# Two transformer-like blocks in one launch: five places where the order or the grain of small steps is changed

## The reference, cut to what matters

```python
def reference(x, c, ..., mem_2, ...):
    x = first_block(x, c, w_ada, b_ada, w_in, ...)     # below
    return second_block(x, mem_2, w_in_2, ...)         # below

# first block: six vectors of 1024 from silu(c) @ w_ada + b_ada scale, shift and gate what follows
#   h = norm(x) * (1 + scale) + shift;  in-projection of h
#   retention: 4 heads of 128, rotary, per-head decay, head norm, gate
#   gated linear attention: 4 heads in 2 pairs
#   out-projection, norm, MLP with squared ReLU (1024 -> 4096 -> 1024), norm

# second block:
#   proj = h @ w_in_2, split into z, xbc, dt, u_s5, x_rg, g_rg
def ssd_mixer(z, xbc, dt_raw, conv_w, conv_b, dt_bias, a_log, d_skip, norm_w):
    xbc = silu(causal_dwconv(xbc, conv_w, conv_b))     # 4 taps, per channel, along the tokens
    dt  = softplus(dt_raw + dt_bias);  a = -exp(a_log)
    # per chunk of 128 tokens and head: y = (C B' * exp(segment sums of dt*a)) (x*dt)
    #   + C (decayed state), state carried from chunk to chunk; then + x*d_skip, * silu(z), norm
def s5_mixer(u, lam_re, lam_im, log_step, b, c, d_skip, glu_w, glu_b):
    lam_bar = exp(lam * step);  b_bar = ((lam_bar - 1) / lam) * b      # complex
    h = linear_scan(lam_bar, b_bar u);  y = gelu(real(c h) + d_skip * u)
    return y * sigmoid(y @ glu_w + glu_b)
#   RG-LRU mixer; y = concat(ssd, s5, rg) @ w_out_2, norm, cross-attention, norm, MLP, norm
```

## Time and profile before

| | |
|---|---|
| median of three executions | 2831.02 us |
| lowest and highest | 2827.89, 2831.63 us |
| profiled execution, its own time | 2834.3 us |
| its span in the profile | 2832.5 us |
| mean granted clock of TensorE | 0.971 |
| TensorE busy | 2664.0 us (94%), 13340 matmuls |
| TensorE's weight loads busy | 1375.1 us (49%) |
| VectorE busy | 1434.6 us (51%) |
| ScalarE busy | 966.8 us (34%) |
| GpSimd busy | 686.9 us (24%) |
| HBM | 64 GB/s over the span |

### The profile page before, as it was taken

One profiled execution on the slowest core, in us unless ns is written; L12 is line 12 of the kernel. 1 busy time (PEld: TensorE's weight loads), 2 busy tenths in 40 slices (PEclk: granted clock), 3 DMA queues, 4 the chain that ended last, 5 costly groups with the idle time before them and its releaser, 6 DMA issues.

```text
span 2832.5 us, 34001 instructions
## 1 busy us (share of the span) xinstructions
PE 2664.0 (94%) x13340; PEld 1375.1 (49%) x13340; DVE 1434.6 (51%) x2282; ACT 966.8 (34%) x1152; POOL 686.9 (24%) x355
## 2 busy tenths in 40 slices
PE   6999999888999999999988899888999999999998
PEld 3677766443444444444454444344544444444443
DVE  6255354567554445675574749663336622222225
ACT  3434315025223322234254253253325332322231
POOL 1211024012212212321542222116103711221222
PEclk9999999998999999999979999999999999999999
DMA  7311131202111111221021230100011101111111
GB/s 297 117 61 68 42 120 45 90 30 90 32 58 60 46 44 60 75 90 45 31 90 49 86 115 30 45 30 31 32 43 60 60 30 60 60 53 37 60 45 60
DMA packets 55589, 182.44 MB, mean 64 GB/s; under 512 B 3952, under 2 KB 4368, under 8 KB 48016
## 3 DMA queue, kind: packets, MB, share of 16 engines
q1 hardware_dynamic: 47136, 138.89, 14.2%
q10 hardware_dynamic: 8304, 41.46, 4.0%
HBM read 170.90 MB, written 9.45 MB: 64 GB/s over the span
## 4 chain that ended last, share of the span: by engine, by line
PE 76%; DVE 10%; ACT 4%; POOLq 3%; DVEq 3%; issue 2%; POOL 1%; DMA 1%; ACTq 1%; SPq 0%
PE PS L682 22%; PE PS L683 22%; PE PS L684 22%; DVE XT L2081 1%; POOLq L611 1%; POOLq L609 1%; PE PS L724 1%; PE PS L1424 1%; ACT WB L1491 1%; POOL WB L555 1%; DVEq L2080 1%; PE PS L1397 1%; ACT WS L1493 1%; PE PS L973 1%; DMA Hf<-in_w_ada 1%
## 5 line engine op out<-in xcount | busy, mean ns | idle before, releaser
L555 POOL TENSOR_TENSOR WB<-WS,WB 128x512 f16<-128x512 f32 (+1 forms) x264 | 489.2, 1886 | 1869.7 <-ACT WS L1493 1869.4
L682 PE MATMUL PS<-XT,WB 128*128 128x512 f16 x1568 | 599.1, 382 | 16.6 <-DVE Hf L2079 11.4
L683 PE MATMUL PS<-XT,WB 128*128 128x512 f16 x1568 | 599.2, 382 | 0.0
L684 PE MATMUL PS<-XT,WB 128*128 128x512 f16 x1568 | 598.8, 382 | 0.0
L682 PE MATMUL PS<-WB,Hf 128*128 128x512 f16 x1440 | 551.7, 383 | 20.7 <-DVEq L2084 6.4
L683 PE MATMUL PS<-WB,Hf 128*128 128x512 f16 x1440 | 550.9, 383 | 0.0
L684 PE MATMUL PS<-WB,Hf 128*128 128x512 f16 x1440 | 550.2, 382 | 0.0
L2079 DVE CAST Hf<-S 128x512 f16<-128x512 f32 x172 | 145.0, 843 | 491.0 <-ACT S L1739 386.0
L1491 ACT ACTIVATE WB<-WS 128x2048 f16<-128x2048 f32 (+3 forms) x118 | 212.6, 1802 | 504.2 <-PE PS L684 469.2
L2437 DVE SCALAR_TENSOR_TENSOR R<-PS,R 128x512 f32<-128x512 f32 x208 | 143.0, 691 | 260.8 <-PE PS L684 253.3
L682 PEld LDWEIGHTS PS<-XT,WB 128*128 128x128 f16 x1568 | 154.4, 98 | 204.4 <-DVE Hf L2079 7.1
(11 more groups left out here) (381 smaller groups left out, 2762.6 us busy)
## 6 DMA issues: line engine op xcount, KB each, us to landing
WS<-in_w_ff SPq DMA_DIRECT2D x32, 1024.0 KB, 5.1
WS<-in_mlp_w SPq DMA_DIRECT2D x32, 1024.0 KB, 5.2
WS<-in_w_mix SPq DMA_DIRECT2D x20, 1024.0 KB, 4.9
Hf<-in_w_ada ACTq DMA_DIRECT2D x12, 1024.0 KB, 6.0
Hf<-in_w_ada SPq DMA_DIRECT2D x8, 1024.0 KB, 11.0
WS<-in_w_out SPq DMA_DIRECT2D x8, 1024.0 KB, 5.0
R<-in_x SPq DMA_DIRECT2D x4, 1024.0 KB, 10.1
R<-in_x ACTq DMA_DIRECT2D x2, 2048.0 KB, 7.8
```

Of the source, the lines that this page charges most:

```text
L555: op = pool.tensor_tensor(WB[:, slot, 1, at:at + n], WS[:, hf, i * n:(i + 1) * n], WB[:, slot, 0, at:at + n], ALU.subtract)
L682: pe.matmul(o, ah, bh, start=(first and k == 0), stop=False, skip_group_check=True)
L683: pe.matmul(o, ah, bl, start=False, stop=False, skip_group_check=True)
L684: mm = pe.matmul(o, al, bh, start=False, stop=(last and k == n - 1), skip_group_check=True)
```

## The change

Five edits, all of them in the order or the grain of small steps; the arithmetic and the data are the same.

1. In the opening VectorE does partial_sum(1), with its signal ada_acc, before mod_diagonal(2) and modc_ready.
2. The wait for head h's gated rows and their eight transposes become a function. For heads 0 to 2 they are called behind job 0 of the next iteration, ahead of late_total, and no longer behind job 7 of their own; for head 3 they stay where they were.
3. In the first MLP the folds (and the wait for lambda_out with its signal) move from behind pieces 6 and 7 of the first chunk to behind pieces 4 and 6 of the second. VectorE's first turn of the loop is written out for that; the loop has two turns for this MLP.
4. The SSD's tile 3 is convolved by halves of 512 tokens, the first half as soon as the first of its two jobs is copied. Its SiLU is applied by halves too, the first half within the loop; the SiLU of tile 2 moves between the two copies of tile 3. silu_done counts five per group, TensorE waits for the fifth only at chunk 4. The decay matmuls and their exponential move ahead of the group's last job and of its copy.
5. At the end of S5 VectorE does both products first, then scalings and rests by halves of the tokens, with a signal (s5_rows) for each. TensorE no longer waits at barrier 5; it only signs it, and waits for s5_rows in the output projection before its first job of each half of the tokens.

```diff
@@ TensorE
+            def gated_rows(h):
+                pe.wait_ge(mix_v, mv_ret(h, "gated"))
+                for g in range(2):
+                    b = side_bank()
+                    for u in range(4):
+                        n = (4 * g + u) * P
+                        mm = pe.transpose(PS[:, b, u * P:(u + 1) * P], RU["on"][:, n:n + P], IDENT)
+                    side_end(mm)
+
             for h in range(-1, 4):
...
                     if j == 0:
+                        if h >= 1:
+                            gated_rows(h - 1)
                         late_total(h + 1)
...
                             for jj in range(4):
                                 project_job(wide(C["gla0"]), jj)
-                        pe.wait_ge(mix_v, mv_ret(h, "gated"))
-                        for g in range(2):
-                            b = side_bank()
-                            for u in range(4):
-                                n = (4 * g + u) * P
-                                mm = pe.transpose(PS[:, b, u * P:(u + 1) * P], RU["on"][:, n:n + P], IDENT)
-                            side_end(mm)
+                            gated_rows(h)
...
                     if t in (0, 4):
                         pe.wait_ge(w_split, c0 + n + 1)
+                    if c0 == C["o2_0"] and n == 0 and t in (0, 4):
+                        pe.wait_ge(s5_rows, 1 + t // 4)
...
+                    if g == 0 and j == 7:
+                        pe.wait_ge(dt_ready, 1)
+                        b = side_bank()
+                        for i, m in enumerate((GT, LE, ONES)):
+                            mm = pe.matmul(PS[:, b, 64 * i:64 * i + 64], m, ADT.rearrange("p t h -> p (t h)"),
+                                           start=True, stop=True, skip_group_check=True)
+                        side_end(mm)
                     columns_job(W, j // 2, j % 2)
                 used_jobs.extend([J[0]] * (2 - g))
-                if g == 0:
...
-                pe.wait_ge(silu_done, 4 * g + 2)
+                pe.wait_ge(silu_done, 5 * g + 2)
...
                 def scores(t):
+                    if t == 4:
+                        pe.wait_ge(silu_done, 5 * g + 5)
...
-            barrier(5)
+            reads_done()
@@ ScalarE
                         act.activation(RAW[n % 2][:, hf * HALF:(hf + 1) * HALF], PS[:, b, :],
                                        ACT.Copy, scale=UNSCALE).then_inc(evac[b], 1)
-                    if f >= 1:
-                        act.wait_ge(conv_done, n)
-                        act.activation(SSD_T[f - 1], SSD_T[f - 1], ACT.Silu).then_inc(silu_done, 1)
+                        if n == 3 and hf == 0:
+                            K[0] = SIDE["dec"]
+                            b = side_in()
+                            act.activation(DECAY.rearrange("p a t h -> p (a t h)"), PS[:, b, 0:192],
+                                           ACT.Exp).then_inc(evac[b], 1)
+                        if f >= 1 and hf == (f < 3):
+                            act.wait_ge(conv_done, n)
+                            act.activation(SSD_T[f - 1], SSD_T[f - 1], ACT.Silu).then_inc(silu_done, 1)
+                    if f == 3:
+                        act.wait_ge(conv_half, g + 1)
+                        act.activation(half(SSD_T[3], 0), half(SSD_T[3], 0), ACT.Silu).then_inc(silu_done, 1)
...
                 act.wait_ge(conv_done, 4 * g + 4)
-                act.activation(SSD_T[3], SSD_T[3], ACT.Silu).then_inc(silu_done, 1)
+                act.activation(half(SSD_T[3], 1), half(SSD_T[3], 1), ACT.Silu).then_inc(silu_done, 1)
@@ VectorE
             partial_sum(0)
+            partial_sum(1)
+            dve.drain().then_inc(ada_acc, 1)
             mod_diagonal(2)
             dve.drain().then_inc(modc_ready, 1)
-            partial_sum(1)
-            dve.drain().then_inc(ada_acc, 1)
...
                 hidden(0, 0, None if last else s5_setup)
-                with dve.Fori(0, 3) as i:
+                for u in range(0 if last else 2):
+                    hidden((u + 1) % 2, 0, s5_folds if u == 0 else None)
+                    down(0, False)
+                with dve.Fori(0, 3 if last else 2) as i:
...
-                if j == 6:
+            def s5_folds(j):
+                if j == 4:
                     dve.wait_ge(s5_raw_in, 32)
                     fold(S5_SETUP["fold_c"][:, 0, :], S5_SETUP["fold_c"][:, 1, :], 10, 11)
-                if j == 7:
+                if j == 6:
                     fold(S5_SETUP["step_c"][:, 0, :], S5_SETUP["step_c"][:, 1, :], 13, 14)
                     dve.wait_ge(lambda_out, 32)
                     dve.sem_inc(s5_p, 1)
...
+            def convolve(dst, raw, weight, bias, signal=None, at=0, end=SEQ):
+                dve.drain()
+                dve.tensor_scalar(dst[:, at:end], raw[:, at:end], weight(3), bias, ALU.mult, ALU.add)
                 for s in range(1, 4):
                     dve.drain()
-                    dve.scalar_tensor_tensor(dst[:, s:], raw[:, 0:SEQ - s], weight(3 - s), dst[:, s:],
+                    a = max(at, s)
+                    dve.scalar_tensor_tensor(dst[:, a:end], raw[:, a - s:end - s], weight(3 - s), dst[:, a:end],
                                              ALU.mult, ALU.add)
...
+                    if f < 3:
+                        convolve(SSD_T[f], RAW[n % 2], weight, bias, conv_done)
+                    else:
+                        convolve(SSD_T[f], RAW[n % 2], weight, bias, conv_half, 0, HALF)
+                        need_wide(dve, ssd_wide(g, f) + 1)
+                        convolve(SSD_T[f], RAW[n % 2], weight, bias, conv_done, HALF, SEQ)
...
-                y = S5_Y[f].rearrange("p (a c) -> p c a", a=2)
-                hi, lo = (H[:, l, 4 + f, :].rearrange("p (c a) -> p c a", a=2) for l in range(2))
-                dve.tensor_scalar(hi, y, M_SCALE, None, ALU.mult)
-                dve.drain()
-                dve.scalar_tensor_tensor(lo, y, M_SCALE, hi, ALU.mult, ALU.subtract)
+            for part in range(2):
+                c = slice(part * 256, (part + 1) * 256)
+                parts = [(S5_Y[f].rearrange("p (a c) -> p c a", a=2)[:, c, :],
+                          *(H[:, l, 4 + f, :].rearrange("p (c a) -> p c a", a=2)[:, c, :] for l in range(2)))
+                         for f in range(2)]
+                for y, hi, lo in parts:
+                    dve.tensor_scalar(hi, y, M_SCALE, None, ALU.mult)
+                dve.drain()
+                for y, hi, lo in parts:
+                    dve.scalar_tensor_tensor(lo, y, M_SCALE, hi, ALU.mult, ALU.subtract)
+                dve.drain().then_inc(s5_rows, 1)
             barrier(5)
```

32 lines of the change are left out of this document (9 added, 23 removed).

## The result

The changed kernel took 2816.62 us, the median of five executions (2815.94 to 2818.05); the kernel before took 2831.63 beside it (2827.89 to 2833.67). The ratio is 0.9949, with a 95% interval of 0.9938 to 0.9960: 14.4 us less, between 11 and 18. Forecast were 13.5 us less and 2817.5, with a range of 2810 to 2826. One execution in all the timings of this document, of f67_2, took 8478 us and is left out of its time.

The account below looks back on a forecast made before the run. TensorE, busy 94% of the span, bounds the kernel, so only its idle time and the slow stretches behind can be saved. -0.9 + 0.5 - 6.4 - 4.8 - 1.9 = -13.5 us, giving a median of 2817.5 us, range 2810 to 2826.

Parts of the forecast that it names:

- The opening: VectorE's partial_sum(1) moved ahead lets the weight pieces come earlier: gain 0.9 us, bounds 0 and 1.1.
- Gated rows: Transposes behind the next head's first job: head 1's pieces 1.2 us late, cost 0.5 us, bounds 0 and 1.2.
- Folds: MLP folds moved away from GpSimd's splitting: 8.6 us saved, 2.2 charged, net 6.4, bounds 3 and 8.6.
- SSD: Tile 3 by halves starts the first exponential earlier: 2.7 us in group 0, 2.1 in group 1, sum 4.8.
- The new wait: In the MLP, piece 7 held by GpSimd's splitting delays the down jobs: about 2 us at the sixth, 2.2 charged.
- sign (4): The SSD groups' first segment exponentials come 2.7 and 2.1 us nearer to the end of their last job.
- S5 output: Output by halves makes the first half ready earlier: gain 1.9 us, wait 4.5 instead of 6.4, bounds 1.2 and 3.6.
- A: Rival in the MLP: second fold meets GpSimd's splitting, the folds' gain becomes 0, time 2824 us; chance 0.12.
- B: Rival: later waits absorb half the SSD and S5 gains, 2821 us, with A 2828; chance 0.12, a third with A.
- C: Rival: moved transposes become the release at all three heads, costing 25 us against 14 saved, 2842 us; chance 0.04.
- D: Rival: VectorE late from the longer straight program, and halves cost extra drains: 2831 us, no change; chance 0.06.

Follow-up runs that it names:

- f67_2: The kernel after with the folds behind pieces 6 and 7 of the second chunk, not 4 and 6: 2826.96 us (median of eleven), ratio 0.9987 to the kernel before.
- u_opening: The kernel after with partial_sum(1) put back behind mod_diagonal(2): 2817.67 us, ratio 0.9955 to the kernel before.
- only_gated2: The kernel before with only the gated rows' transposes moved: 2831.76 us, ratio 1.0003 to the kernel before.
- u_gated: The kernel after with the gated rows' eight transposes put back behind job 7 of their own iteration: 2815.07 us, ratio 0.9943 to the kernel before.
- u_folds: The kernel after with the folds put back behind pieces 6 and 7 of the first chunk: 2823.42 us, ratio 0.9973 to the kernel before.
- f24_2: The kernel after with the folds behind pieces 2 and 4 of the second chunk, not 4 and 6: 2812.97 us, ratio 0.9935 to the kernel before.
- u_ssd: The kernel after with tile 3 convolved whole, ScalarE's order and decay matmuls as before: 2819.00 us, ratio 0.9955 to the kernel before.

## Why the prediction was right

The time, 2816.62 against 2817.5, and the sum, 14.4 against 13.5, were right. The mechanism was right at the folds, the SSD and the opening, which bring most of it; that the sum came within 1 us is in part luck, since the SSD was put 1.9 us too small and the S5 output 0.8 too large. Part by part:

- **The opening:** forecast 0.9, shown 0.91 by u_opening.
- **Gated rows:** forecast a cost of 0.5, within 0 and 1.2; shown 0 within what can be read (only_gated2's ratio 1.0003, whose interval of 0.9995 to 1.0012 doesn't exclude 0.5 us by itself; u_gated against the kernel after in the table -0.12 at the heads and -0.34 behind). The stalls of 2.20 us stayed at heads 0 and 2, and the pieces of head 1 came 1.2 late as forecast. The term was mis-sized: the scores of 2.03 us that stand between cover the lateness of 1.2 entirely, and TensorE loses nothing across head 1.
- **Folds:** forecast 8.6 less 2.2, 6.4; shown 6.33 in the trace, and 6.8 by u_folds' ratio. By its own numbers the loss at half clock was 2.3, not 2.5 (5.11 less 2.8), which changes little: f24_2, with no wait left there, stands at -8.72. Where the folds run came out 3.4 us earlier than the times I gave, but with the distance to the splitting forecast (0.3). The new wait stood at two down jobs (0.36 and 1.69 us), behind the held piece 7, and was 2.0 us; f24_2 took it away and gained 2.35. That an operation of VectorE's is held for GpSimd's whole instruction, on which this sum stood, is shown by f67_2.
- **SSD:** forecast 2.7 and 2.1, shown 3.3 and 3.3. The step that was too small at group 0 is ScalarE's: I counted one table load, the shorter SiLU and the order, 2.7; the exponential of the decays and the load in front of it, 1.6 together, left the path as well, against 0.5 for the SiLU of the first half that now stands on it and 0.6 for the decay matmuls ahead of the job. That gives 3.2. My sign (4) contradicted my sum here: the last job ends 0.8 later by my working, so from its end the exponential should have come 3.5 nearer, not 2.7; it was 3.9. At the first exponential of group 1 the gain was 2.15 us, as forecast, and another 1.2 followed at the chunks behind, with slow stretches of other lengths. The bounds (2.5 to 6.5) were just missed, at 6.7, and by the ratios of u_ssd the part is worth 1.7 to 3.4 at the end.
- **S5 output:** forecast 1.9 and a wait of 4.5; shown a wait of 4.75 (1.67 less than before), of which 1.08 were left behind the half clock. The lower bound named the strided halves at 0.5 and 0.8 as its reason; they took 0.385 and 0.65 each, and the reason is the clock. In other traces with this edit 1.4 to 2.5 stand in the same column.
- **The profile against the median:** I took the 3.3 us by which the profiled execution stood above its median as a constant. It was most likely in the lengths of slow stretches of that execution, 3 us at the heads. The forecast of the median doesn't hang on it.

Of the rivals, A is real as a mechanism and didn't occur: 0.3 us were enough, though piece 7's subtraction was caught as forecast. With B it would come to 2827 by its own terms, not 2828. B occurred in a part: 2.6 us of 6.7 were given back between u_ssd and the kernel after, where the slow stretches differ and not, as I had it, through ScalarE's rounding. C's condition, TensorE stalled at all three heads, was not met. D is excluded: the folds' program cost nothing (-0.02 us over the 585 us of the MLP behind them).

The Trainium skill's rule (SBUF — State Buffer, "SBUF: two separate sides") that the loser of the shared ports is blocked for the other's whole instruction agrees with f67_2's two rows. Its 2.66 us for each switch of ScalarE's table (ScalarE: Activation LUTs, "What ACT_TABLE_LOAD costs") is not what this trace shows: load, exponential, load and SiLU in a row went from 1403.84 to 1407.84, 4.0 us, with 1.28 for each load, and the idle time of 1.13 behind them is what was left of the job.

## What to carry to other kernels

In this kernel long VectorE work on SBUF tensors belongs where GpSimd is idle, and the question of a move is which short operation now stands beside GpSimd's instruction: here moving two folds by two pieces more was worth another 2.4 us. Before a table load or a function is moved on ScalarE, list everything between the last input and the first output that others wait for; here undoing either half of ScalarE's new order (2.8 and 3.0 us) cost nearly as much as undoing the whole edit (3.3). A gain of 1 to 3 us in one pair of profiles can be the length of slow stretches: take a second trace of the same program, and compare the same stretch in several traces, of kernels with and without the edit, before it is credited to the code.

## What the runs showed that I had not expected

- The stretch at half clock behind the stall of head 0 was 6.8 us long in one of fourteen traces (the kernel before's) and 3.4 in the other thirteen, with the transposes in either place; at head 2 it was 3.4 or none. In the SSD's group 0 the clock stood at 0.50 for 24 us in the kernel before and at 0.79 over the same work after:

```profile
1426.00:1450.00 24.00, 20.21 (x55) 11.97 (x56) 16.39 (x26) 17.53 (x13) 15.82 (x12) 0.50 0.26 89
```

```profile
1413.30:1437.30 24.00, 14.73 (x53) 8.23 (x54) 19.44 (x32) 17.42 (x13) 16.02 (x12) 0.79 0.26 88
```

  That accounts for 5.5 of the 12 us by which TensorE was less busy, and seems to have cost little: TensorE waits for VectorE there at either clock, and the nine traces with the whole new SSD code had 10 to 17 us of half clock at this work and stand between -3.2 and -4.2 in the table, the one with 17 at -3.2 and the three with 10 at -3.3 and -3.4.
- Beside GpSimd's instruction, VectorE's scaling and gating of a PSUM bank (one operand in PSUM, one in SBUF) took its usual 0.69 us (725.57), between two operations on SBUF tensors that were held 4.39 and 3.60.
- TensorE's first matmul came between 17.7 and 19.4 us after the span's start in the traces of one and the same program, by when its weights had landed: more than the opening's edit is worth.
